# The eight gate columns of a hybrid decoder block: taken into the second projection block (520 columns) in place of a product of their own

## The reference, cut to what matters

```
xn    = rms_norm(x)
proj  = xn @ w_in        # w_in: 2048 x 10248
q,k,v,o of 4 mLSTM heads | 8 gate logits (input and forget gate of 4 heads) | q,k,v of 8 MoBA heads | 2 x 2048 branch gates
h_a   = mlstm(q, k, v, gates)  * sigmoid(o)
h_b   = causal attention of 8 heads with QK-norm and ALiBi
merged = sigmoid(g_A) * (h_a @ W_A) + sigmoid(g_B) * (h_b @ W_B)
x = x + merged @ W_out
x = x + relu(rms_norm(x) @ W_up)^2 @ W_down
```

## Time and profile before

| what | value |
|---|---|
| median of 3 runs | 1366.26 us (1365.49 to 1367.26) |
| profiled execution, its time | 1367.06 us |
| profiled execution, its span | 1365.2 us |
| PE busy | 1359.2 us, 100% of the span |
| PEld busy | 1141.8 us |
| DVE busy | 835.5 us |
| ACT busy | 632.0 us |
| granted TensorE clock, mean | 1.000 (2.4 GHz) |
| DMA, share of 16 engines (main queue) | 56.7% |

### The profile page before, as it was taken

One profiled execution on the slowest core, in us unless ns is written; L12 is line 12 of the kernel. 1 busy time (PEld: TensorE's weight loads), 2 busy tenths in 40 slices (PEclk: granted clock), 3 DMA queues, 4 the chain that ended last, 5 costly groups with the idle time before them and its releaser, 6 DMA issues.

```text
span 1365.2 us, 17369 instructions
## 1 busy us (share of the span) xinstructions
PE 1359.2 (100%) x6543; PEld 1141.8 (84%) x6543; DVE 835.5 (61%) x989; ACT 632.0 (46%) x777; POOL 15.2 (1%) x35
## 2 busy tenths in 40 slices
PE   9999999999999999999999999999999999999999
PEld 7788888888888888888888888888888888888887
DVE  4778678545675666689865655444445655644443
ACT  4655555464444444444544444333334444434332
POOL 1010000000000000000000000000000000000000
PEclk9999999999999999999999999999999999999999
DMA  8555654555655655555655555555555555555552
GB/s 280 173 197 179 201 175 155 185 160 179 247 185 185 210 185 190 183 200 171 216 189 188 190 193 195 185 188 201 196 185 187 190 190 192 192 189 187 199 198 92
DMA packets 132551, 258.74 MB, mean 190 GB/s; under 512 B 6250, under 2 KB 8340, under 8 KB 132244
## 3 DMA queue, kind: packets, MB, share of 16 engines
q1 hardware_dynamic: 130336, 257.97, 56.7%
q10 hardware_dynamic: 2164, 0.09, 0.1%
HBM read 255.94 MB, written 2.10 MB: 189 GB/s over the span
## 4 chain that ended last, share of the span: by engine, by line
PE 98%; DVE 1%; DMA 0%; issue 0%; ACT 0%; SPq 0%; DVEq 0%; ACTq 0%
PE ps L933 23%; PE ps L935 23%; PE ps L934 23%; PE ps L948 17%; PE ps L952 9%; PE ps L964 1%; DVE w_lo L617 0%; DVE ps L635 0%; DMA rows<-in_x_dram 0%; PE ps L1071 0%; PE ps L984 0%; PE ps L1014 0%; PE ps L1033 0%; PE ps L1034 0%; PE ps L1032 0%
## 5 line engine op out<-in xcount | busy, mean ns | idle before, releaser
L617 DVE TENSOR_TENSOR w_lo<-raw,w_hi 128x1024 fp32r<-128x1024 f32 x480 | 584.9, 1224 | 485.3 <-ACT w_hi L365 483.2
L365 ACT ACTIVATE w_hi<-raw 128x1024 fp32r<-128x1024 f32 x480 | 506.3, 1062 | 639.7 <-PE ps L935 451.6
L948 PE MATMUL ps<-xT,w_hi 128*128 128x512 f32 x1024 | 319.2, 395 | 0.0
L933 PE MATMUL ps<-w_hi,xT 128*128 128x512 f32 x640 | 254.2, 397 | 0.7 <-DVE w_lo L617 0.7
L935 PE MATMUL ps<-w_hi,xT 128*128 128x512 f32 x640 | 249.5, 390 | 0.0
L934 PE MATMUL ps<-w_lo,xT 128*128 128x512 f32 x640 | 249.1, 389 | 0.0
L952 PEld LDWEIGHTS ps<-xT,w_lo 128*128 128x128 f32 x1024 | 190.0, 188 | 43.9
L952 PE MATMUL ps<-xT,w_lo 128*128 128x256 f32 x1024 | 198.9, 278 | 0.0
L948 PEld LDWEIGHTS ps<-xT,w_hi 128*128 128x128 f32 x1024 | 157.2, 189 | 1.4
L933 PE MATMUL ps<-w_hi,merged 128*128 128x512 f32 x384 | 149.5, 389 | 0.2 <-DVE merged L820 0.2
L933 PE MATMUL ps<-w_hi,branch 128*128 128x512 f32 x384 | 149.5, 389 | 0.0
(11 more groups left out here) (174 smaller groups left out, 673.5 us busy)
## 6 DMA issues: line engine op xcount, KB each, us to landing
raw<-in_w_in_dram SPq DMA_DIRECT2D x79, 1024.0 KB, 5.1
raw<-in_w_up_dram SPq DMA_DIRECT2D x64, 1024.0 KB, 5.3
raw<-in_w_down_dram SPq DMA_DIRECT2D x64, 1024.0 KB, 5.0
raw<-in_w_out_dram SPq DMA_DIRECT2D x16, 1024.0 KB, 5.0
raw<-in_w_branch_b_dram SPq DMA_DIRECT2D x8, 1024.0 KB, 5.1
raw<-in_w_branch_a_dram SPq DMA_DIRECT2D x8, 1024.0 KB, 5.0
rows<-in_x_dram SPq DMA_DIRECT2D x8, 256.0 KB, 7.7
rows<-in_x_dram SPq DMA_DIRECT2D x1, 2048.0 KB, 8.1
```

The source lines that it names most:

```text
L365: act.activation(w_hi[:, k % RING, :, :], raw[:, k // 2, KH * (k % 2):KH * (k % 2) + KH, :], ACT.Copy).then_inc(hi_made, 1)
L617: dve.tensor_tensor(w_lo[:, k % RING, :, :], raw[:, k // 2, KH * (k % 2):KH * (k % 2) + KH, :], w_hi[:, k % RING, :, :].bitcast(F32), ALU. ...
L933: pe.matmul(o, hi, w_hi[:, s, i, :], start=first, stop=False)
L948: return pe.matmul(ps[:, q0 + j, :], w_hi[:, s, i, P * j:P * j + P], xT[:, t, :, :].rearrange("p a c -> p (a c)"), start=t == 0, stop=t == ...
```

## The change

The gate columns become the first eight columns of the second query block. Block 0 now loads the queries of heads 4 to 7, block 1 loads 520 columns: the 8 gate columns and the queries of heads 0 to 3. `raw`, `w_hi` and `w_lo` get 520 columns in each slot; every other block uses the first 512 of them. A bank of PSUM holds 512 fp32 columns, so in block 1 (`gate_rows`) each matmul of 512 columns becomes two, of 264 and of 256 columns, into banks 2 and 3 for the first token half and 6 and 7 for the second. The product L984, its copy L430, the sums L992, the load, split, buffers and constants of the old path are gone. DVE takes `if_nat` out of the banks of block 1 at H = 21. The buffer `g_parts` moves into `branch`. Block 3 waits for `if_nat`, since it writes banks 2 and 3 next.

```diff
-W_IN_COLS = [B_COL + N * i for i in range(6)] + [N * i for i in range(6)]
+W_IN_COLS = [B_COL + N, IF_COL] + [B_COL + N * i for i in range(2, 6)] + [N * i for i in range(6)]
+GATES = 1
+NW = N + IF
...
-P_IF_SUM, P_IF_ADD, P_IF_ROWS, P_IF_COLS = 9, 14, 25, 48
+P_IF_ROWS, P_IF_COLS = 25, 48
...
-        raw = sb("raw", [P, RAW, KL, N])
-        w_hi = sb("w_hi", [P, RING, KH, N], F32R)
-        w_lo = sb("w_lo", [P, RING, KH, N], F32R)
+        raw_wide = sb("raw", [P, RAW, KL, NW])
+        hi_wide = sb("w_hi", [P, RING, KH, NW], F32R)
+        lo_wide = sb("w_lo", [P, RING, KH, NW], F32R)
+        raw, w_hi, w_lo = raw_wide[:, :, :, 0:N], hi_wide[:, :, :, 0:N], lo_wide[:, :, :, 0:N]
...
-        wif = sb("wif", [P, KT, IF])
-        wif2 = sb("wif2", [P, KT * 16 + 112], F32R)
-        g_parts = wif2[:, 0:S]
+        g_parts = branch[:, 7, 0, :]
...
-                sp.dma_start(raw[:, k, :, :], src).then_inc(landed[k], 16)
+                dst = raw_wide[:, k, :, :] if isinstance(blk, int) and blk == GATES else raw[:, k, :, :]
+                sp.dma_start(dst, src).then_inc(landed[k], 16)
...
-                    load(b, k, w_in_t[:, KL * k:KL * k + KL, W_IN_COLS[b]:W_IN_COLS[b] + N])
+                    load(b, k, w_in_t[:, KL * k:KL * k + KL, W_IN_COLS[b]:W_IN_COLS[b] + (NW if b == GATES else N)])
...
-            pool.memset(pick[:, :, :].bitcast(F32), 0.0)
-            link(pool.memset(add2[:, :], 0.0))
+            link(pool.memset(pick[:, :, :].bitcast(F32), 0.0))
...
-            link(pool.affine_select(out=add2[:, :], in_=add2[:, :], compare_op=ALU.not_equal, fill=1.0, base=0,
-                                    pattern=[[-1, IF]], channel_multiplier=1))
...
-                act.dma_start(wif[:, :, :], w_in_t[:, :, IF_COL:IF_COL + IF]).then_inc(wif_landed, 16)
...
-                act.activation(w_hi[:, k % RING, :, :], raw[:, k // 2, KH * (k % 2):KH * (k % 2) + KH, :],
+                wide = isinstance(blk, int) and blk == GATES
+                src, dst = (raw_wide, hi_wide) if wide else (raw, w_hi)
+                act.activation(dst[:, k % RING, :, :], src[:, k // 2, KH * (k % 2):KH * (k % 2) + KH, :],
                                ACT.Copy).then_inc(hi_made, 1)
...
-                    last = act.activation(dst[:, m, :], ps[:, 2 * (g % 2) + m, :], func, scale=rstd[:, m:m + 1])
+                    if g == GATES:
+                        last = act.activation(dst[:, m, :].rearrange("p (a c) -> p a c", a=2),
+                                              ps[:, 2 + 4 * m:4 + 4 * m, IF:IF + S], func, scale=rstd[:, m:m + 1])
+                    else:
+                        last = act.activation(dst[:, m, :], ps[:, 2 * (g % 2) + m, :], func, scale=rstd[:, m:m + 1])
...
-                    c = P * (g % 4)
-                    last = act.activation(sq[:, P * g:P * g + P], ps[:, 2 * (b % 2) + g // 4, c:c + P], ACT.Square,
+                    bank, c = 2 * (b % 2) + g // 4, P * (g % 4)
+                    if b == GATES:
+                        bank, c = 2 + 4 * (g // 4) + g % 4 // 2, IF + P * (g % 2)
+                    last = act.activation(sq[:, P * g:P * g + P], ps[:, bank, c:c + P], ACT.Square,
                                           scale=rstd[:, g // 4:g // 4 + 1], accum_out=ssq[:, g:g + 1])
...
-                if H == 7:
-                    act.wait_ge(wif_landed, 16)
-                    act.wait_ge(if_dve, 1)
-                    act.activation(wif2[:, 0:KT * 16].rearrange("p (t c) -> p t c", c=16)[:, :, 0:IF], wif[:, :, :],
-                                   ACT.Copy).then_inc(if_hi, 1)
-                if H == P_IF_SUM + 5:
-                    act.wait_ge(if_pe, 1)
-                    act.activation(if_raw[:, :, :], ps[0:16, 7, :].rearrange("p (a t) -> p a t", a=2),
-                                   ACT.Copy).then_inc(if_act, 1)
...
-                if k == 7:
-                    jobs(7)
...
-                dve.tensor_tensor(w_lo[:, k % RING, :, :], raw[:, k // 2, KH * (k % 2):KH * (k % 2) + KH, :],
-                                  w_hi[:, k % RING, :, :].bitcast(F32), ALU.subtract).then_inc(lo_made, 1)
...
-                if H == 8:
-                    dve.wait_ge(if_hi, 1)
-                    w = wif2[:, 0:KT * 16].rearrange("p (t c) -> p t c", c=16)
-                    dve.tensor_tensor(w[:, :, IF:16], wif[:, :, :], w[:, :, 0:IF].bitcast(F32),
-                                      ALU.subtract).then_inc(if_lo, 1)
...
-                if H == P_IF_ADD + 5:
-                    dve.wait_ge(if_pe, 2)
+                if H == 8 * GATES + 13:
+                    dve.wait_ge(kept[GATES], 1)
                     dve.memset(g_parts.bitcast(F32), 0.0)
                     for m in range(M):
-                        last = dve.tensor_scalar(if_nat[:, m, :], ps[:, 7, IF * m:IF * m + IF], rstd[:, m:m + 1], None,
+                        last = dve.tensor_scalar(if_nat[:, m, :], ps[:, 2 + 4 * m, 0:IF], rstd[:, m:m + 1], None,
                                                  ALU.mult)
                     last.then_inc(if_dve, 1)
...
-            dve.memset(wif2[:, :].bitcast(F32), 0.0).then_inc(if_dve, 1)
...
+            def gate_rows(k):
+
+                pe.wait_ge(lo_made, 8 * GATES + k + 1)
+                cols_of = (slice(0, IF + S), slice(IF + S, NW))
+                for m in range(M):
+                    for i in range(KH):
+                        t, s = 2 * k + i, k % RING
+                        hi, lo = (xT[:, t, a, P * m:P * m + P] for a in range(2))
+                        out_of = (ps[:, 2 + 4 * m, 0:IF + S], ps[:, 3 + 4 * m, IF:IF + S])
+                        for o, c in zip(out_of, cols_of):
+                            pe.matmul(o, hi, hi_wide[:, s, i, c], start=t == 0, stop=False)
+                        for o, c in zip(out_of, cols_of):
+                            pe.matmul(o, hi, lo_wide[:, s, i, c], start=False, stop=False)
+                        for o, c in zip(out_of, cols_of):
+                            last = pe.matmul(o, lo, hi_wide[:, s, i, c], start=False, stop=t == KT - 1)
+                last.then_inc(w_used, 1)
...
-                if p == P_IF_SUM:
-                    pe.wait_ge(if_lo, 1)
-                    for t in range(KT):
-                        last = pe.matmul(ps[:, 7, :], wif2[:, 16 * t:16 * t + P],
-                                         xT[:, t, :, :].rearrange("p a c -> p (a c)"), start=t == 0, stop=t == KT - 1)
-                    last.then_inc(if_pe, 1)
-                if p == P_IF_ADD:
-                    pe.wait_ge(if_act, 1)
-                    pe.wait_ge(c_pool, 2)
-                    for m in range(M):
-                        for a in range(2):
-                            last = pe.matmul(ps[:, 7, IF * m:IF * m + IF], if_raw[:, a, P * m:P * m + P], add2[:, :],
-                                             start=a == 0, stop=a == 1)
-                    last.then_inc(if_pe, 1)
                 if p == P_IF_ROWS:
-                    pe.wait_ge(if_dve, 2)
+                    pe.wait_ge(if_dve, 1)
...
+                if b == GATES + 2:
+                    pe.wait_ge(if_dve, 1)
                 for k in range(8):
                     if b == 0:
                         pe.wait_ge(xl_made, k + 1)
-                    half_rows(b, k, 2 * (b % 2), xT, 2 * k, start=k == 0, stop=k == 7)
+                    if b == GATES:
+                        gate_rows(k)
+                    else:
+                        half_rows(b, k, 2 * (b % 2), xT, 2 * k, start=k == 0, stop=k == 7)
```

More of the change, by code:

```diff
@@ L137, in build @@
         pick = sb("pick", [P, NA, P], F32R)
-        add2 = sb("add2", [16, IF])
         mix_rows = sb("mix_rows", [16, P])
@@ L157, in build @@
         if_nat = sb("if_nat", [P, M, IF])
-        if_raw = rows[0:16, 0, OA:OA + 512].rearrange("p (a t) -> p a t", a=2)
         gi = rows[0:NA, 0, OA + 512:OA + 1024].rearrange("p (a t) -> p a t", a=2)
@@ L189, in build @@
         kept = [sem("kept0"), sem("kept1")]
-        mix_landed, c_landed, wif_landed, c_pool, g_turned, g_kept, ones_made = (
-            sem(s) for s in ("mix_landed", "c_landed", "wif_landed", "c_pool", "g_turned", "g_kept", "ones_made"))
+        mix_landed, c_landed, c_pool, g_turned, g_kept, ones_made = (
+            sem(s) for s in ("mix_landed", "c_landed", "c_pool", "g_turned", "g_kept", "ones_made"))
         first_landed = sem("first_landed")
@@ L200, in build @@
             sem(s) for s in ("ss_made", "rms_made", "nat_scaled", "qk_turned", "qk_kept"))
-        if_hi, if_lo, if_pe, if_act, if_dve = (sem(s) for s in ("if_hi", "if_lo", "if_pe", "if_act", "if_dve"))
+        if_pe, if_act, if_dve = (sem(s) for s in ("if_pe", "if_act", "if_dve"))
         sc_made, low_made, p_made, p_scaled, p_turned, pt_kept, hb_made, hb_hi, hb_lo = (
@@ L465, in jobs @@
                         dst, g = (qTb, G_Q) if i < 2 else (kTb, G_K)
-                        act.activation(dst[:, 4 * (i % 2):4 * (i % 2) + 4, :], src, ACT.Copy,
```

(29 more changed lines are left out.)

10 lines of the change are left out of this document (4 added, 6 removed).

## The result

| | before | after |
|---|---|---|
| median, four runs each | 1365.88 us (1365.27 to 1367.26) | 1384.16 us (1384.06 to 1386.35) |
| span of the profiled execution | 1365.2 us | 1382.4 us |

The ratio is 1.0137, 95% interval 1.0123 to 1.0152: 18.3 us slower, where 1.6 us faster was forecast, and 17 us above the range.

A forecast was written before the change was run, and what follows sets the result against it. PE, busy 100%, was taken as the bound: 1.71 - 4.99 = -3.28 us alone, but the DVE and ACT loop allows only -1.64, so 1366.26 - 1.6 = 1364.6 us; range 1362.4 to 1367.2.

The forecast's parts named there:

- rival D: The new width and 2080-byte pitch slow all 480 splits or all PE streams; 1% would be 13 us; 0.12 with C.
- Rival C: Weight loads set the pace of block 1's short matmuls: +9.3 us, 1375.6; chance 0.12 together with D.
- The sign that the prediction gave for D: In the changed profile, steps of 512 columns above 0.2273 us outside block 1.
- The paragraph on what costs nothing: Costed at nothing: `if_nat` and `kept[1]` waits, two-piece operands on DVE (1226 against 1224 ns), ACT's bank reads, loads of 520 columns.
- PE's sum, -3.28 by p = 16: PE alone: 4.99 us of work and wait leave, 1.71 us come with block 1's pairs, so -3.28 us.
- DVE and ACT allow -1.64 by p = 40: At block 5's start the DVE and ACT loop gets only 1.64 us earlier, so PE waits for `w_lo`.
- some 0.9: PE's forecast wait for `w_lo` at p = 24, the start of block 3, in us.
- the old wait of block 0: PE's 0.7 us wait for `w_lo` at block 0's last half-block, of which 0.20 us goes with L426.
- Rival A: PE's sum holds in full, without waits after block 1: 3.3 us faster, 1363.0; chance 0.17.
- B: DVE gains nothing, from the gates' new place or a next wait; p = 40 near 130.5, time 1366.0; chance 0.15.
- The place of `if_nat`, +0.34 in DVE's loop: Memset and `if_nat` move from H = 19 to H = 21, between two `w_lo` splits: +0.34 us.

The follow-up runs named there:

- F1: The changed kernel with slots of 4352 bytes and rows 512 columns apart in every block but block 1, two small buffers moved into `attn`: 1363.84 us.
- G1: The kernel before with 128 bytes of padding between `raw` and `w_hi`, moving all that PE reads together: 1365.63 us.
- F4: The kernel before with `w_hi` and `w_lo` both moved by 256 bytes: 1365.45 us.
- G4: The kernel before with only `raw`, which PE never reads, at a pitch of 520 columns: 1365.55 us.
- H4: F1 with DVE's memset and `if_nat` one half-block earlier, at H = 20 in place of 21: 1363.23 us.
- E5: The kernel before with `w_hi` 32 bytes further, `w_lo` 96 and what lies behind them 128: 1401.85 us.
- G2: The kernel before with 128 bytes of padding behind `w_lo`, moving the activations and all that follows but not the weights: 1388.04 us.
- F3: The kernel before with `w_hi` and `w_lo` both moved by 128 bytes: 1387.79 us.
- G3: The kernel before with only `w_lo` moved by 128 bytes and all behind it by 256: 1389.85 us.
- H3: The kernel before with `w_hi` moved by 128 bytes, `w_lo` and all else behind it by 256: 1378.29 us.

## Why the prediction was wrong

**The step that failed** is the weight given to rival D: "Nothing in the rows speaks for it. I put it with C." Right: nothing in the rows did, since every row of before has one layout, and such rows can't speak against it either. "1% on PE's streams would be 13 us" stood there as a price; measured were 2.4% (226.7 to 232.1 ns) in the down projections, 0.4% in the up projections (178.44 to 179.17 us) and 20 us in all. The sign that the prediction gave for D, steps of 512 above 0.2273 elsewhere, is the one that came. The paragraph on what costs nothing asked of spread pieces only what DVE pays, by its 1226 against 1224 ns, and DVE indeed pays nothing (1225 ns a split after, 1224 before). The same edit changed the addresses of every operand that the full engine reads, and for PE the question was not asked. The bound from above was thus missing where one nanosecond counts 4128 times. The runs show in its place: a step of 512 streamed weight columns takes 226.7 ns where weights and activations start at the same offset within 256 bytes, and with the rows 2080 bytes apart it takes 232.1, a loss of some 20 us that swallows the gain of 1.5.

**What the layout cost**, from after against F1, which differ in the layout alone (two small buffers moved with it): from the first stream to the first up projection 664.06 - 9.83 = 654.23 us against 653.63 - 10.15 = 643.48, 10.8 us; two down projections of 4.16 and two up projections of 0.73; sum 20.5, the medians say 20.3.

**What the change itself brings**, where F1 shows it bare. Timeline of PE in F1, first stream, block 1, starts of blocks 2, 3 and 5:

```profile
10.15 0.47 PE L926 MATMUL ps<-w_hi,xT 128*128 128x512 f32 x1
...
36.50 0.40 PE L964 MATMUL ps<-w_hi,xT 128*128 128x264 f32 x2
...
59.18 0.41 PE L968 MATMUL ps<-w_hi,xT 128*128 128x264 f32 x2
...
60.03 0.47 PE L926 MATMUL ps<-w_hi,xT 128*128 128x512 f32 x1 [0.44 <-DVE w_lo L616]
...
82.79 0.47 PE L926 MATMUL ps<-w_hi,xT 128*128 128x512 f32 x1 [0.76 <-DVE w_lo L616]
...
127.45 0.47 PE L926 MATMUL ps<-w_hi,xT 128*128 128x512 f32 x1 [0.30 <-DVE w_lo L616]
```

- *PE's sum, -3.28 by p = 16.* From the first stream: 60.03 - 10.15 = 49.88 against 64.97 - 11.61 = 53.36, -3.48. Right; the pair was put too high, 22.68 / 95 = 0.2387 measured for 0.2451, so +1.10 us in place of +1.71, and 0.44 us of it went into a wait at p = 16 that I had expected only from block 3 on.
- *DVE and ACT allow -1.64 by p = 40.* 127.45 - 10.15 = 117.30 against 130.72 - 11.61 = 119.11: -1.81. Three more executions with this order of work and 226.7 ns steps, G1, F4 and G4, give 119.09 to 119.11, so the difference is clear of noise. At p = 24 "some 0.9": the row has 0.76 of idle time, and from one stream to the next 1.15 us pass where 0.23 would do, 0.92. The waits of L926 on `w_lo` in F1 (waits view: total, times, longest) are 2.0 us. 0.46 of it is the old wait of block 0, which was put at 0.5; the 1.5 behind it was put at 1.6, though it begins at block 2 and block 4 has none:

```profile
PE ps L926 <- DVE w_lo L616: 2.0, 4, 0.8
```

- *The sum.* 1363.84 - 1365.38 = -1.5 us, forecast -1.6 (from a median of three that stood 0.8 too high). With the layout kept at multiples of 256 bytes the forecast comes out by its own steps, but for the split of the waits. Rival A, the whole -3.3 us by p = 40, falls in F1; so does B, which had -0.2 there.
- *The place of `if_nat`, +0.34 in DVE's loop.* H4 takes it back to H = 20, and PE's waits shrink. Waits view and timeline of PE in H4, blocks 3 and 5:

```profile
PE ps L926 <- DVE w_lo L616: 1.5, 4, 0.5
```

```profile
82.12 0.47 PE L926 MATMUL ps<-w_hi,xT 128*128 128x512 f32 x1 [0.29 <-DVE w_lo L616]
...
126.78 0.47 PE L926 MATMUL ps<-w_hi,xT 128*128 128x512 f32 x1 [0.33 <-DVE w_lo L616]
```

  From the first stream, at 9.94, that is 116.84, 0.46 less than F1, where the term had 0.34: it held, somewhat larger. The reason is on DVE, first F1, then H4: in F1 the memset of 0.27 us pushes the second `w_lo` back, in H4 it stands in idle time and the two follow without a gap.

```profile
67.54 1.23 DVE L616 TENSOR_TENSOR w_lo<-raw,w_hi 128x1024 fp32r<-128x1024 f32 x1 [3.29 <-ACT w_hi L366]
68.77 0.27 DVE L698 MEMSET branch<- 128x256 f32 x1
69.10 1.22 DVE L616 TENSOR_TENSOR w_lo<-raw,w_hi 128x1024 fp32r<-128x1024 f32 x1
```

```profile
66.44 0.27 DVE L698 MEMSET branch<- 128x256 f32 x1 [2.43 <-ACT attn L374]
67.30 2.36 DVE L616 TENSOR_TENSOR w_lo<-raw,w_hi 128x1024 fp32r<-128x1024 f32 x2 [0.44 <-ACT w_hi L366]
```

- *In after itself* this gain is there too, under the loss. From its first stream p = 16 starts 50.01 us on, against 53.36 in before. Its waits on `w_lo` are fewer than forecast, because a block of 96 steps at 0.2314 to 0.2321 takes PE 22.2 to 22.3 us, almost as long as DVE's and ACT's loop of 22.34:

```profile
PE ps L921 <- DVE w_lo L611: 1.0, 3, 0.4
```

- *Rival C, weight loads set the pace*, had most of the chance of slower, and was wrong: 95 pairs, two full loads each, at 0.2396 us. By the Trainium skill's rule that the prediction weighed ("TensorE: Matmul & The Clock Gate", "The mechanism") the loads of block 1 would stand bare. The same section also has a load for the background weight buffer pulled ahead of running matmuls, which the prediction left out. A row of 190 matmuls of 264 and 256 columns at 0.12 us each disagrees with the bare loads once more.
- *A reading that was off.* The prediction called the 0.7 us for `w_lo` PE's one wait of half a microsecond or more on another compute engine. There is a longer one, on POOL, right at the start; it lies ahead of the stretch of the change and touches no term. Waits view of before:

```profile
PE ps L1071 <- POOL ident L298: 1.5, 1, 1.5
```

The lowest median is H4's, 1363.23 us: 0.19% less than before [0.10% to 0.28%], and 20.9 us less than the change as it was made.

## What to carry to other kernels

Where PE is the full engine, look at where its operands start before and after an edit of any buffer's size: a pad, a wider row or one more small tile ahead of them moves all that lies behind, and this trace has the same instructions 1% to 4% slower for it. For fp32r products with stationary activations and streamed weights, as in most of this kernel, keep both at the same offset within 256 bytes (slots and pitches in multiples of 256 bytes do it). In a forecast, a term for "nothing else is touched" needs a reason for each engine that reads what the edit re-lays, the bound engine first; rows that all share one layout are none.

## What the runs showed of the hardware

- The pace of back-to-back fp32r matmuls of 512 columns depends on how their operands' start addresses lie to each other within 256 bytes: 226.7 ns where all agree, up to 235.5 ns (E5) where they don't, at a granted clock of 1.00. Shown: moving everything together costs nothing (G1), 256 costs nothing (F4), moving the activations or the weights by 128 costs the same 5.7 ns (G2, F3), and ACT's, DVE's and the DMAs' source array has no part in it (G4).
- It is no plain function of one offset: +6.6, +2.2, +5.7 and +6.6 ns for 32, 64, 128 and 192 bytes of both weight arrays, and the charges of the two arrays don't add up (G3 and H3 against F3). Nor is it paid by the shifted stream alone (G3: 235.5, 234.4 and 230.0 ns for a trio of which the middle one is shifted). Whether a stream disturbs the weight load beside it or the stream behind it stays open: no run here separates the two.
- Where the weights are stationary (the up projections) other offsets are the good ones: 192 bytes made each of them 1.8 us shorter than the aligned layout (176.64 against 178.44), 64 bytes 0.95, while the down projections lost. A layout with its own offset for each stage was not tried.
- The Trainium skill, in "SBUF — State Buffer", section "Operand start alignment", asks of an fp32 operand a start at a multiple of 4 bytes, and says that this is about what is legal, not about speed. Each layout here keeps it, and they lie up to 36 us apart.
- The start of a run is not fixed, because the granted clock rises at different times. The first record of full clock in the stored trace stands at 10.38 us of the span in before and at 6.39 in after; the 24 warm-up matmuls take 4.09 and 2.84 us, and while the clock is low they follow each other at 213 ns in place of 112, as at 1.2 in place of 2.4 GHz. All 18 traces fall into these two groups: full clock from 4.8 to 7.3 us and warm-ups of 2.84 us, or from 10.4 to 11.1 us and 4.0 to 4.4 us. The times of one and the same kernel before lie in two groups too, around 1365.4 and 1367.2; the profiled executions of before, G1 and F4 (late clock) took 1367.06, 1367.28 and 1367.55, that of G4 (early) 1365.55. So 1.8 us, more than this change is worth, depends on which group a single run falls into, and a few runs can't tell a change of this size. Why the clock rises late in some executions no run shows.
